# ScalarE's copy and VectorE's addition of the PSUM halves put ahead of the next weight tile's split, in a kernel of two transformer layers in split float32

## The reference, cut to what matters

```
proj = rmsnorm(x) @ w_in                  # then stick-breaking, indexed and memory attention
merged = sum_n sigmoid(gl_n + b_n) * (o_n @ w_branch[n])
x = x + merged @ w_out
u = causal_dwconv(rmsnorm(x) @ w_up);  g, val = split(u)
x = x + (silu(g) * val) @ w_down
x = x + rms_norm(gla_mixer(rms_norm(x)))  # gated linear attention
x = x + rms_norm(mla_mixer(rms_norm(x)))  # latent attention
```

## Time and profile before

| | |
|---|---|
| median of 3 runs | 2647.68 us (2646.3 to 2649.38) |
| the profiled execution | 2647.79 us, its span 2646.0 us |
| TensorE busy with matmuls | 2570.5 us, 97% of the span |
| VectorE busy | 1666.9 us, 63% |
| ScalarE busy | 1310.4 us, 50% |
| granted TensorE clock, mean | 0.983 |
| HBM traffic | 167 GB/s over the span |

### The profile page before, as it was taken

One profiled execution on the slowest core, in us unless ns is written; L12 is line 12 of the kernel. 1 busy time (PEld: TensorE's weight loads), 2 busy tenths in 40 slices (PEclk: granted clock), 3 DMA queues, 4 the chain that ended last, 5 costly groups with the idle time before them and its releaser, 6 DMA issues.

```text
span 2646.0 us, 40634 instructions
## 1 busy us (share of the span) xinstructions
PE 2570.5 (97%) x14860; PEld 2239.3 (85%) x14860; DVE 1666.9 (63%) x2063; ACT 1310.4 (50%) x1686; POOL 107.4 (4%) x82
## 2 busy tenths in 40 slices
PE   7999999999999999999999999999999997999998
PEld 6888888888888888888888888888888886988886
DVE  6754654566695577777577757785465847655454
ACT  6545444544444555555355535554444554444454
POOL 3000000000000001000000000010001111000000
PEclk9999999999999999999999999999899998999998
DMA  6564666456565656666666666666454553544353
GB/s 205 184 183 136 191 189 188 132 176 175 161 190 144 191 176 189 180 185 187 187 184 183 190 189 185 179 190 180 130 166 128 172 186 108 144 122 128 112 163 107
DMA packets 545507, 442.94 MB, mean 167 GB/s; under 512 B 31241, under 2 KB 542753, under 8 KB 544866
## 3 DMA queue, kind: packets, MB, share of 16 engines
q1 hardware_dynamic: 545186, 441.00, 56.4%
q0 software_dynamic: 192, 0.18, 0.1%
HBM read 439.02 MB, written 2.10 MB: 167 GB/s over the span
## 4 chain that ended last, share of the span: by engine, by line
PE 86%; DVE 7%; ACT 4%; issue 1%; POOL 1%; DMA 1%; SPq 0%; DVEq 0%; ACTq 0%; POOLq 0%
PE blk L648 79%; DVE weight L1678 2%; DVE arena L1678 1%; PE pa L901 1%; ACT weight L1112 1%; ACT arena L1326 1%; PE pa L712 1%; DVE xT L1678 1%; DVE u L1752 1%; DMA weight_raw<-in_w_mem_kv_dram 0%; PE pa L992 0%; DMA weight_raw<-in_w_branch_dram 0%; DVE small L1915 0%; DVE arena L2278 0%; PE pa L703 0%
## 5 line engine op out<-in xcount | busy, mean ns | idle before, releaser
L1678 DVE TENSOR_TENSOR weight<-weight_raw,weight 128x1024 fp32r<-128x1024 f32 (+2 forms) x836 | 1019.5, 1224 | 828.2 <-ACT weight L1112 824.7
L1112 ACT ACTIVATE weight<-weight_raw 128x1024 fp32r<-128x1024 f32 (+2 forms) x836 | 870.4, 1045 | 1033.4 <-PE blk L648 990.6
L648 PE MATMUL blk<-u,weight 128*128 128x512 f32 x5312 | 948.5, 341 | 17.9 <-DVE u L1752 14.5
L648 PEld LDWEIGHTS blk<-u,weight 128*128 128x128 f32 x5312 | 817.2, 190 | 144.0 <-issue 18.0
L648 PE MATMUL blk<-h,weight 128*128 128x512 f32 (+1 forms) x5344 | 929.2, 335 | 4.1 <-DVE h L1678 4.1
L648 PEld LDWEIGHTS blk<-h,weight 128*128 128x128 f32 x5344 | 806.1, 189 | 117.1 <-issue 5.0
L648 PE MATMUL blk<-weight,h 128*128 128x256 f32 (+4 forms) x1952 | 312.1, 321 | 0.0
L648 PEld LDWEIGHTS blk<-weight,h 128*128 128x128 f32 x1952 | 278.4, 190 | 31.7 <-issue 0.3
L648 PE MATMUL blk<-weight,u 128*128 128x512 f32 (+5 forms) x1152 | 210.1, 344 | 4.6 <-DVE weight L1678 4.6
L648 PEld LDWEIGHTS blk<-weight,u 128*128 128x128 f32 x1152 | 181.4, 201 | 29.5 <-DVE weight L1678 5.4
L1678 DVE TENSOR_TENSOR arena<-arena,blk 128x512 f32<-128x512 f32 (+1 forms) x142 | 96.2, 677 | 9.4 <-ACT arena L1164 9.4
(11 more groups left out here) (229 smaller groups left out, 1167.6 us busy)
## 6 DMA issues: line engine op xcount, KB each, us to landing
weight_raw<-in_w_in_dram SPq DMA_DIRECT2D x216, 512.0 KB, 3.6
weight_raw<-in_w_up_dram SPq DMA_DIRECT2D x344, 256.0 KB, 3.2
weight_raw<-in_l_gla_w_in_dram SPq DMA_DIRECT2D x96, 512.0 KB, 3.8
weight_raw<-in_w_down_dram SPq DMA_DIRECT2D x80, 512.0 KB, 3.4
weight_raw<-in_w_branch_dram SPq DMA_DIRECT2D x48, 512.0 KB, 4.0
weight_raw<-in_l_mla_w_in_dram SPq DMA_DIRECT2D x48, 512.0 KB, 3.9
weight_raw<-in_w_mem_kv_dram SPq DMA_DIRECT2D x32, 512.0 KB, 4.3
weight_raw<-in_w_out_dram SPq DMA_DIRECT2D x32, 512.0 KB, 3.4
```

The lines of the kernel that those rows point to most:

```text
L648: mm = nc.tensor.matmul(to, lhsT, rhs, start=(kt == 0 and m == 0), stop=(kt == ph.bt - 1 and m == len(ops) - 1))
L1112: nc.scalar.activation(weight_hi[:, r, 0:nk, 0:cols], weight_raw[:, r, 0:nk, 0:cols], ACT.Copy).then_inc(hi_made, 1)
L1678: return nc.vector.tensor_tensor(out_, a, b, op)
```

## The change

At a block's last tile ScalarE first copies the PSUM half (`lift`), then splits the next weight tile, then does `final`; VectorE first waits for the lifted half and joins, and then makes the low part of the split. At all other tiles the work and its order are as they were. No instruction is added or removed. Lines below the change in the kernel's ScalarE part stand one line lower than before (L1172 is now L1173, L1678 is L1679).

```diff
                     act.wait_ge(tile_used, i * ph.period + (t + 1))
+                    b, r = i * (ph.period // ph.bt) + j // ph.bt, (ph.b0 + j // ph.bt) % PSUM_RING
+                    if j % ph.bt == ph.bt - 1 and lift is not None:
+                        lift(b, r).then_inc(block_lifted if ph.merged else block_out, 1)
                     if not isinstance(i, int) or t + i * ph.period + RING < plan.tiles:
                         split_hi(t + RING, ph.period, i)
                     if j % ph.bt == ph.bt - 1 and lift is not None:
-                        b, r = i * (ph.period // ph.bt) + j // ph.bt, (ph.b0 + j // ph.bt) % PSUM_RING
-                        lift(b, r).then_inc(block_lifted if ph.merged else block_out, 1)
                         if final is not None:
                             act.wait_ge(block_joined, b + (ph.j0 + 1))
                             final(b).then_inc(block_out, 1)
...
                         dve.wait_ge(tile_used, i * ph.period + (t + 1))
                         out_of_psum(b, r)
-                    if not isinstance(i, int) or t + i * ph.period + RING < plan.tiles:
-                        split_lo(t + RING, i, ph.period)
                     if j % ph.bt == ph.bt - 1 and join is not None:
                         dve.wait_ge(block_lifted, b + (ph.l0 + 1))
                         join(ph, b, r)
+                    if not isinstance(i, int) or t + i * ph.period + RING < plan.tiles:
+                        split_lo(t + RING, i, ph.period)
```

## The result

The changed kernel takes 2620.88 us (median of 4 runs, 2612.9 to 2622.9) against 2646.99 us for the kernel before (4 runs beside it): a ratio of 0.990, 95% interval 0.9877 to 0.9923, 26 us less. The forecast was 17 us less. (Three single executions of the later groups took 2828, 4711 and 5575 us; ratios and mean clocks leave them out, and the medians shift by at most half a us with them.)

The account below looks back on a forecast made before the run. TensorE, busy 2570.5 of 2646.0 us, was taken as the bound, with its short waits on chains what could shrink. Waits 14.8 less cost 0.8 plus clock 3.4 made 17.4 us: 2630.4 us, range 2625 to 2642.

Parts of the forecast that it names:

- What bounds the kernel, and one block's end: TensorE's waits on chains over other engines bound it, at most 75 us; at a block's end tanh starts 1.4 us earlier.
- The waits: Across the phases whose chains pass a block's end, TensorE's waits shrink by 14.8 us in sum.
- gate1: Attention of 2 x 4 heads: waits for the copy behind the tanh and for VectorE's normalising shrink, 4.4 us.
- gate0: Three TensorE waits in this phase, whose chains pass tiles 7, 11 and 15, shrink by 2.7 us in sum.
- gate2: TensorE waits in this phase, whose chains pass tiles 3 and 11, shrink; with 0.1 at tile 7, 2.3 us.
- the latent attention's gates: ScalarE's silu there comes 1.14 us earlier, and TensorE's waits for the copy behind it shrink, 2.3 us in sum.
- up to down: Three TensorE waits for `h` between these phases shrink: 0.5 of the longest and the two of 0.4, 1.3 us.
- glaout's end: At the end of this phase ScalarE starts the squares 1.54 us after the tile instead of 2.95: 1.4 us less.
- What the change costs: Low parts come later at 184 block ends, uncovered only in glagate: between 0 and 1.35 us lost, 0.8 taken.
- The table load: A load ahead of the tanh takes 1.28 us, so gains are small: 0.14 at gate1's tile 3, 1.07 at gate2's.
- The clock: Two half-speed stretches of TensorE behind gate1's waits go, 3.4 us back; nothing counted for mlagate1.
- more comes back: Rival, chance 0.07: the half-speed stretch in mlagate1 goes too, another 3.4 us, giving 2627 us.

Follow-up runs that it names:

- later groups: Further runs on the same chips, with the changed kernel unchanged again beside the kernel before: 2622.64 us, ratio 0.9909, and 2622.75 us, ratio 0.992.
- filling waits: Unused transposes put into TensorE's waits: kernel before 2642.81 us, ratio 0.9993; changed kernel 2614.71 us, 0.9901; new order in phases with chains only 2618.49 us, 0.9905.

## Why the prediction was off

**What bounds the kernel, and one block's end: right.** What moved by the change is in TensorE's waits and in the clock behind them. The bound of 75 us was too low, though: TensorE's busy time holds some 35 us that only half speed costs (half of 70.2). The lift, split, join and tanh start at 0.02, 0.5, 0.65 and 1.46 us behind the block's last tile, where 0, 0.58, 0.61 and 1.54 were forecast; the copy behind the tanh came 1.5 earlier (1.4 forecast).

**The waits: right, a little short.** Term by term, idle time of the two profiles before against the three after: gate1 7.0 to 2.3, 4.7 less (forecast 4.4); gate0 4.2 and 4.6 to 1.1 to 1.3, 3.2 (2.7); gate2 3.3 to 1.0 and 1.3, 2.1 (2.3); the latent attention's gates 2.5 at mlaout's head and 1.1 to 1.4 at qnope1, less 0.3 in mlagate0 and 0.8 in mlagate1, 2.6 (2.3); up to down 1.2 (1.3); glaout's end 1.4 (1.4); krope 0.4 (0.35). These sum to 15.6 against 14.8. With 0.6 in places that I didn't count (0.35 behind the last tile, 0.2 in branch1) and 0.85 more waiting in the first phase, where waits for DMA scatter by a us, it is 15.4 on average. The 13.8 of the first pair hit the sum because its first phase waited 1.0 and its glagate 1.2 us more than before.

**What the change costs: right in place, but nothing net.** The low part of glagate's waits 3.15 instead of 1.83, 1.32 more; I had the bounds 0 and 1.35 and took 0.8. Other waits in the phase are shorter for it: glagate idles 5.8 and 7.9 us in the profiles before and 6.6 to 7.1 after, so on average nothing was lost. The half-speed stretch there doubled in two of three profiles, as allowed for.

**The table load: right.** L703, behind a tile with a table load, went from 1.7 to 0.7, 1.0 for the 1.07 forecast by the row. At tile 3 of gate1, with a load of 1.28 us ahead of it, the tanh started 2.97 us behind the tile before and 2.88 after, 0.1 earlier (0.14 forecast).

**The clock: this step failed.** It reads "I count both back: 3.4 us" and, of mlagate1, "the idle time there is split in two but stays 2 us long, so I count nothing". The two stretches did go, and by TensorE's 6.6 us in them they were worth 3.3. But in all, TensorE's busy time at half speed fell from 70.2 and 87.3 us to 59.0, 62.9 and 62.0: 5.6 us of loss in the first pair, 8.7 on average, where the sum had 3.4. (All runs' mean clocks, which count half speed in idle time too, put it at 46.1 and 45.3 us before and at 38.3 and 41.1 after on the same chips, 7.8 and 4.2 less.) Three things were missed. Mlagate1's stretch goes (1.7 to 3.0 us): the waits left there, 1.17 and 0.62 us, are each short, and it was wrong to add them up. One profile is one draw: the kernel before has two or three such stretches in gate1 and at times one in gate0 (3.4 us each in the records), and I took the two of one execution as all there are. And at the head of latent TensorE is busy at half speed for 8.5 to 10.6 us after, where it was for 10.5 and 13.4. That the clock gives back more was a rival in the prediction, "more comes back", with a chance of 0.07. Its mechanism, mlagate1's stretch, is what happened; its time, 2627 us, is still 6 above the measured one.

**The rest is pace,** of which the prediction knew nothing: 3.9 us between the first two profiles. There, 13.8 of idle time, 5.6 of clock and 3.9 of pace make 23.3 of the 25.1 us by which the spans differ. On average over the profiles they are 15.4, 8.7 and 3.1, 27.2 of 28.2. For the medians of all runs, which differ by 23 to 26 us, how much is pace is not known, since it is known for the profiled executions alone.

## What to carry to other kernels

Where two engines prepare the next weights and also end a block, put the block's end first on both, or on the one whose queue holds the join: done on the lifting engine alone the same idea made this kernel slower. When a change shortens waits of 2 to 3 us of a TensorE that is otherwise always busy, count the half-speed stretches behind every one of them as part of its price, 1.7 us for each 3.4 in which TensorE is busy and nothing for those in which it idles, and look at more than one execution before counting them. Time given back inside a chain of waits is not time gained: filling waits paid in full where one wait stood alone (glagate), and in small part at the head of latent, where four follow each other.

## What the runs showed of the hardware

- TensorE's two paces at full clock, 2.773 and 2.831 us for a tile of 16 matmuls, 3.4 to 3.6 ns per matmul, steady over hundreds of us and changing, as a rule, at interruptions. With 244 to 499 of some 715 tiles at the slower one, it explains up to 14 us between executions of kernels that do the same work. What chooses the pace stays open.
- Half-speed stretches stood behind single waits of 1.8 us (glagate, clock record from 2075.6 to 2079.0) and more, and not always: the wait of 2.47 us in gate1 had none behind it with the change in mlagate1 alone (clock 1.00 from 826 to 830), and the same wait in the kernel before had one; the wait of 3.3 us at the head of down2 had none in the first profile, and 3.2 us there had 6.8 us at half speed behind it in the second. Behind the single waits of 1.3 us and less that the change left in gate1 and mlagate1 there was none in any of the profiles. The Trainium skill (TensorE: Matmul & The Clock Gate, HAM oscillation) says that idle gaps bring the half clock back; the filled waits bear that out for this kernel.
- Half speed costs only where TensorE works: at the head of latent 20.5 us of clock record held 10.5 us of matmuls, and a mean granted clock counts the whole.
